# Second mixer of a two-layer transformer block: latent normalisation in two parts, modulation pieces spread over the projections, scan parts ahead of the score maxima

## The reference, cut to what matters

```
def odd_mixer(t, w_in, ...):                       # t: 256 x 1024
    proj = t @ w_in                                # 256 x 704: u 256, c_q 256, c_kv 128, k_r 64
    y_c = s5_ssm(u, ...)                           # scan over 256 tokens, 1024 complex states
    y_d = mla_attention(c_q, c_kv, k_r, ...)
    return concatenate([y_c, y_d], -1) @ w_out

mla_attention:
    q  = rmsnorm(c_q, q_norm) @ w_uq               # 256 x (6 heads x 192)
    kv = rmsnorm(c_kv, kv_norm) @ w_ukv            # 256 x (6 heads x 256)
    ... rope on 64 of the query's columns and on k_r; softmax attention, 6 heads, 2 blocks of 128 queries
s5_ssm:
    bu = u @ bbar; x_t = a * x_(t-1) + bu_t; y = Re(c x) + d u; z = gelu(y); z * sigmoid(z @ w_glu + b)
```

## Time and profile before

| what | before |
|---|---|
| median of 3 runs | 2066.13 us |
| the profiled execution's own time | 2075.66 us |
| its span | 2073.9 us |
| TensorE matmul busy | 1913.7 us (92%) |
| GpSimd / ScalarE / VectorE busy | 1347.5 / 930.1 / 722.7 us |
| memory read | 342.03 MB, 165 GB/s over the span |
| mean granted TensorE clock | 0.968 |

### The profile page before, as it was taken

How to read it: one execution, slowest core, us unless ns; L and a number is a source line. 1 busy time by engine, 2 the same in 40 slices (tenths; PEclk the granted TensorE clock), 3 DMA queues, 4 the chain that set the end, 5 groups by cost and what they waited for, 6 DMA issues and landing times.

```text
span 2073.9 us, 28300 instructions
## 1 busy us (share of the span) xinstructions
PE 1913.7 (92%) x9582; PEld 1518.0 (73%) x9582; DVE 722.7 (35%) x1296; ACT 930.1 (45%) x1458; POOL 1347.5 (65%) x780
## 2 busy tenths in 40 slices
PE   7987999889899999888999999899999999899997
PEld 5666788765678878666888776678887776678886
DVE  1375443265421134344111545342113544342112
ACT  5535344443544353544444444544444444544442
POOL 5405899440488869545988783367885883367884
PEclk9999999999999999999999999999999999999999
DMA  7666555547765546323775452245754452245552
GB/s 260 226 215 229 183 184 188 166 152 250 241 216 183 187 137 189 106 94 120 203 212 183 141 169 86 72 142 167 209 189 134 153 162 82 72 138 157 185 189 72
DMA packets 257208, 344.32 MB, mean 166 GB/s; under 512 B 33376, under 2 KB 153056, under 8 KB 257120
## 3 DMA queue, kind: packets, MB, share of 16 engines
q1 hardware_dynamic: 243328, 337.13, 50.8%
q10 hardware_dynamic: 13792, 6.03, 1.7%
HBM read 342.03 MB, written 1.05 MB: 165 GB/s over the span
## 4 chain that ended last, share of the span: by engine, by line
PE 86%; DVE 7%; ACT 2%; DMA 2%; issue 2%; SPq 0%; POOL 0%; ACTq 0%; DVEq 0%
PE bank L1930 24%; PE bank L1932 23%; PE bank L1931 23%; PE bank L2001 3%; PE bank L2450 2%; PE bank L2477 2%; PE bank L2460 2%; PE bank L2012 1%; PE bank L1980 1%; DMA raw<-in_w_mod 1%; PE bank L2167 1%; PE bank L2442 1%; DVE arena L1872 1%; PE bank L2247 1%; DVE small L1838 1%
## 5 line engine op out<-in xcount | busy, mean ns | idle before, releaser
L641 POOL TENSOR_TENSOR wl<-raw,wh 128x1024 fp32r<-128x1024 f32 x300 | 726.1, 2431 | 104.1 <-ACT wh L800 97.9
L1930 PE MATMUL bank<-wh,xh 128*128 128x512 f32 (+2 forms) x1746 | 698.8, 400 | 65.8 <-issue 30.1
L626 POOL TENSOR_TENSOR wl<-raw,wh 128x512 fp32r<-128x512 f32 (+2 forms) x238 | 319.4, 1342 | 595.6 <-ACT wh L662 558.4
L1932 PE MATMUL bank<-wl,xh 128*128 128x512 f32 (+2 forms) x1746 | 682.9, 391 | 0.0
L1931 PE MATMUL bank<-wh,xl 128*128 128x512 f32 (+2 forms) x1746 | 682.0, 391 | 0.0
L800 ACT ACTIVATE wh<-raw 128x1024 fp32r<-128x1024 f32 x270 | 286.5, 1062 | 454.9 <-PE bank L1932 433.5
L1930 PEld LDWEIGHTS bank<-wh,xh 128*128 128x128 f32 x1746 | 335.3, 192 | 145.3 <-issue 56.9
L1932 PEld LDWEIGHTS bank<-wl,xh 128*128 128x128 f32 x1746 | 335.0, 192 | 69.2
L1931 PEld LDWEIGHTS bank<-wh,xl 128*128 128x128 f32 x1746 | 335.7, 192 | 63.3 <-issue 0.7
L662 ACT ACTIVATE wh<-raw 128x1024 fp32r<-128x1024 f32 (+2 forms) x268 | 275.1, 1048 | 217.2 <-PE bank L1932 163.8
L627 POOL TENSOR_TENSOR wl<-raw,wh 128x512 fp32r<-128x512 f32 (+2 forms) x238 | 318.8, 1339 | 0.0
(11 more groups left out here) (316 smaller groups left out, 1669.5 us busy)
## 6 DMA issues: line engine op xcount, KB each, us to landing
raw<-in_w_ffn_in SPq DMA_DIRECT2D x264, 256.0 KB, 3.0
raw<-in_w_in SPq DMA_DIRECT2D x224, 256.0 KB, 2.9
raw<-in_w_mod SPq DMA_DIRECT2D x192, 256.0 KB, 3.9
raw<-in_w_ffn_out SPq DMA_DIRECT2D x132, 256.0 KB, 2.9
raw<-in_l_w_gate SPq DMA_DIRECT2D x88, 256.0 KB, 3.7
raw<-in_l_w_up SPq DMA_DIRECT2D x88, 256.0 KB, 4.4
raw<-in_l_w_down SPq DMA_DIRECT2D x88, 256.0 KB, 2.9
raw<-in_l_w_in SPq DMA_DIRECT2D x48, 256.0 KB, 4.2
```

Source lines behind the costliest of these rows:

```text
L626: nc.gpsimd.tensor_tensor(wl[:, s, 0:h], raw[:, s, 0:h], words(wh)[:, s, 0:h], ALU.subtract)
L641: nc.gpsimd.tensor_tensor(wl[:, s, :], raw[:, s, :], words(wh)[:, s, :], ALU.subtract)\
L1930: mm(dst, x_hi, w_hi, start=first, stop=False, skip_group_check=True)
L1932: return mm(dst, x_hi, w_lo, start=False, stop=last, skip_group_check=True)
```

## The change

Four things change in the second mixer; the rest of the program is as it was.

1. The latents are normed in two parts. The queries' latent (256 columns, all within the first column tile of `in1`) gets its squares, root, scaling, transposes and split before the second column tile of `in1` is taken; the keys' latent (128 columns) follows behind `uq`'s second tile. Its PSUM bank is now bank 5 (before bank 3).
2. Of the nine pieces of `mod1_rope`, six now stand one behind each chunk of `uq` and `ukv`; three are left, and they stand between the sixth and the seventh turn.
3. ScalarE converts the weights of `uq` and `ukv` in between the copies out of PSUM, no longer all ahead of them, and `c_neg` comes behind the keys' latent.
4. VectorE's loop takes its scan part ahead of `mla_top(u + 2)`; the first scan part comes before the split of the keys' latent. On TensorE `drive(2)` stands before the keys' latent is waited for, and `state(0)` behind the first chunk of `ukv`.

```diff
--- before.py
+++ after.py
@@ -230,9 +230,10 @@
     plan.modulation("mod1_in", 1, w_mod[1], 4)
     plan.gemm("in1", a["l1_w_in"], [512, 192])
     plan.modulation("mod1_lat", 1, w_mod[1], 3)
-    plan.gemm("uq", a["l1_w_uq"], [384] * 3)
-    plan.gemm("ukv", a["l1_w_ukv"], [512] * 3)
-    plan.modulation("mod1_rope", 1, w_mod[1], 9)
+    each = {n: (1, w_mod[1]) for n in range(3)}
+    plan.gemm("uq", a["l1_w_uq"], [384] * 3, modulated=each)
+    plan.gemm("ukv", a["l1_w_ukv"], [512] * 3, modulated=each)
+    plan.modulation("mod1_rope", 1, w_mod[1], 3)
...
@@ -410,7 +411,7 @@
         scratch, modbank = bank[6], bank[7]
...
-        lat_bank, ut_bank, drive_bank, state_bank, mla_out = bank[2:4], bank[0], [bank[6], bank[4]], bank[5], bank[3]
+        lat_bank, ut_bank, drive_bank, state_bank, mla_out = (bank[2], bank[5]), bank[0], [bank[6], bank[4]], bank[5], bank[3]
         accb = [[bank[0], bank[1]], [bank[2], bank[3]]]
         gub, gub0 = bank[4:6], bank[0:2]
 
@@ -926,28 +927,41 @@
...
             hi_until(plan.tiles["in1"][1][2][0][0] + RING)
-            for b in range(4):
+
+            def evac_b(b):
                 act.wait_ge(b_tr, b + 1)
                 for i in range(2):
                     nc.scalar.activation(bt[i][:, 2 * b:2 * b + 2, :],
                                          b_bank[b][:, 256 * i:256 * i + 256].rearrange("p (a b) -> p a b", a=2),
                                          ACT.Copy).then_inc(b_ev, 1)
+
+            def latent_root(i):
+                act.wait_ge(lat_ss, i + 1)
+                nc.scalar.activation(lsd[:, 2 * i:2 * i + 2], lsq[:, 2 * i:2 * i + 2], ACT.Sqrt, scale=1.0 / (256, 128)[i],
+                                     bias=eps6).then_inc(lat_std, 1)
+
+            def evac_latent(i):
+                act.wait_ge(lat_tr, i + 1)
+                for k in ((0, 1), (2,))[i]:
+                    nc.scalar.activation(xf[:, k // 2, 256 * (k % 2):256 * (k % 2) + 256],
+                                         lat_bank[i][:, 256 * (k % 2):256 * (k % 2) + 256], ACT.Identity,
+                                         scale=V_("q_norm", k) if k < 2 else V_("kv_norm", 0), bias=zero).then_inc(lat_ev, 1)
+
+            for b in range(3):
+                evac_b(b)
+            latent_root(0)
+            evac_b(3)
+            evac_latent(0)
+            act.wait_ge(ssm_ut, 1)
+            nc.scalar.activation(uT1, ut_bank[:, :].rearrange("p (a b) -> p a b", a=2), ACT.Copy).then_inc(ssm_uev, 1)
+            latent_root(1)
+            tail("in1")
+            hi_until(plan.tiles["uq"][1][2][0][0] + 1)
+            evac_latent(1)
             act.wait_ge(c_in, 32)
             nc.scalar.activation(cz[1], cz[1], ACT.Copy, scale=-1.0).then_inc(c_neg, 1)
-            act.wait_ge(ssm_ut, 1)
-            nc.scalar.activation(uT1, ut_bank[:, :].rearrange("p (a b) -> p a b", a=2), ACT.Copy).then_inc(ssm_uev, 1)
-            tail("in1")
-            act.wait_ge(lat_ss, 1)
-            nc.scalar.activation(lsd[:, 0:2], lsq[:, 0:2], ACT.Sqrt, scale=1.0 / 256, bias=eps6).then_inc(lat_std, 1)
-            nc.scalar.activation(lsd[:, 2:4], lsq[:, 2:4], ACT.Sqrt, scale=1.0 / 128, bias=eps6).then_inc(lat_std, 1)
-            hi_until(plan.tiles["uq"][1][2][0][0] + 1)
-            act.wait_ge(lat_tr, 1)
-            for k in range(3):
-                nc.scalar.activation(xf[:, k // 2, 256 * (k % 2):256 * (k % 2) + 256],
-                                     lat_bank[k // 2][:, 256 * (k % 2):256 * (k % 2) + 256], ACT.Identity,
-                                     scale=V_("q_norm", k) if k < 2 else V_("kv_norm", 0), bias=zero).then_inc(lat_ev, 1)
-            tail("ukv")
             for i in range(3):
+                hi_until(plan.tiles["uq"][i][2][0][0] + RING)
                 act.wait_ge(chunk_used, plan.tiles["uq"][i][2][-1][0] + 1)
...
@@ -970,6 +984,7 @@
                 ins.then_inc(mla_ev, 1)
 
             for i in range(3):
+                hi_until(plan.tiles["ukv"][i][2][0][0] + RING)
                 act.wait_ge(chunk_used, plan.tiles["ukv"][i][2][-1][0] + 1)
...
@@ -1556,26 +1571,34 @@
 
             row_norm("mix1", X)
             take("in1", 0, lambda t, p: v.tensor_copy(proj[:, t, 0:512], p))
-            take("in1", 1, lambda t, p: v.tensor_copy(proj[:, t, 512:704], p))
-            dve.wait_ge(evac, plan.tile_no["in1"] + 2)
-            parts = [(256, 512), (512, 640)]
-            for i, (s, e) in enumerate(parts):
+
+            def latent_squares(i):
+                s, e = ((256, 512), (512, 640))[i]
+                dve.wait_ge(evac, plan.tile_no["in1"] + i + 1)
                 for t in range(TT):
                     x = proj[:, t, s:e]
                     ins = v.tensor_tensor_reduce(q1[:, t, 256 * i:256 * i + e - s], x, x, 1.0, 0.0, ALU.mult, ALU.add,
                                                  lsq[:, 2 * i + t:2 * i + t + 1])
-                    ins.then_inc(lat_ss, 1) if (i, t) == (1, TT - 1) else step(ins)
-            dve.wait_ge(lat_std, 2)
-            step(v.reciprocal(lrs, lsd))
-            settle()
-            for i, (s, e) in enumerate(parts):
+                    ins.then_inc(lat_ss, 1) if t == TT - 1 else step(ins)
+
+            def latent_rows(i):
+                s, e = ((256, 512), (512, 640))[i]
+                dve.wait_ge(lat_std, i + 1)
+                step(v.reciprocal(lrs[:, 2 * i:2 * i + 2], lsd[:, 2 * i:2 * i + 2]))
+                settle()
                 for t in range(TT):
                     x = proj[:, t, s:e]
                     v.tensor_scalar(x, x, lrs[:, 2 * i + t:2 * i + t + 1], None, ALU.mult).then_inc(lat_xn, 1)
+
+            settle()
+            latent_squares(0)
+            latent_rows(0)
             dve.wait_ge(lat_ev, 2)
             split(0, 2, xf[:, 0, :], xt_split)
-            dve.wait_ge(lat_ev, 3)
-            split(2, 1, xf[:, 1, 0:256], xt_split)
+            take("in1", 1, lambda t, p: v.tensor_copy(proj[:, t, 512:704], p))
+            settle()
+            latent_squares(1)
+            latent_rows(1)
 
             def state_space():
 
@@ -1613,7 +1636,10 @@
                     yield
 
             ssm = state_space()
-            for _ in range(6):
+            next(ssm)
+            dve.wait_ge(lat_ev, 3)
+            split(2, 1, xf[:, 1, 0:256], xt_split)
+            for _ in range(5):
                 next(ssm)
             dve.wait_ge(xt_split, split_at["lat1"] + 2)
             dve.wait_ge(evac, plan.tile_no["uq"] + 3)
@@ -1645,11 +1671,11 @@
             for u in range(2 * MH):
                 dve.wait_ge(at_exp, u + 1)
                 v.reciprocal(rinv[:, u % 4:u % 4 + 1], rsum[:, u % 4:u % 4 + 1]).then_inc(at_rinv, 1)
-                if u + 2 < 2 * MH:
-                    mla_top(u + 2)
                 next(ssm)
                 if u % 4 == 3:
                     next(ssm)
+                if u + 2 < 2 * MH:
+                    mla_top(u + 2)
                 if u >= 3 and u % 2:
                     h = u // 2 - 1
                     dve.wait_ge(at_pv, h + 1)
@@ -2255,35 +2281,45 @@
             tile_chunk("in1", 1, 0)
             pe.wait_ge(b_ev, 2)
             b_turn(3)
-            tile_chunk("in1", 1, 1)
-            pe.wait_ge(evac, plan.tile_no["in1"] + 1)
+
+            def latent_turn(i):
+                pe.wait_ge(lat_xn, TT * (i + 1))
+                for k in ((0, 1), (2,))[i]:
+                    for t in range(TT):
+                        ins = tr(lat_bank[i][:, 256 * (k % 2) + P * t:256 * (k % 2) + P * t + P],
+                                 proj[:, t, 256 + k * P:256 + k * P + P], ident)
+                ins.then_inc(lat_tr, 1)
+
+            latent_turn(0)
             pe.wait_ge(b_ev, 4)
             turn(ut_bank, lambda i, t: proj[:, t, i * P:i * P + P], ssm_ut)
+            tile_chunk("in1", 1, 1)
             modulate("mod1_lat")
             pe.wait_ge(ssm_uev, 1)
             pe.wait_ge(b_ev, 8)
             drive(0)
-            pe.wait_ge(lat_xn, 2 * TT)
-            for k in range(3):
-                for t in range(TT):
-                    ins = tr(lat_bank[k // 2][:, 256 * (k % 2) + P * t:256 * (k % 2) + P * t + P],
-                             proj[:, t, 256 + k * P:256 + k * P + P], ident)
-            ins.then_inc(lat_tr, 1)
+
+            def latent_chunk(name, i, shift=0):
+                tile_chunk(name, i, 0, shift)
+                mod_chunk(plan.tiles[name][i][2][0][0] + 1)
+
+            x_ready("lat1", 1)
+            latent_chunk("uq", 0)
+            latent_chunk("uq", 1)
+            latent_turn(1)
             drive(1)
+            pe.wait_ge(evac, plan.tile_no["uq"] + 1)
+            latent_chunk("uq", 2)
+            drive(2)
             x_ready("lat1", 2)
             for i in range(3):
-                if i == 2:
-                    pe.wait_ge(evac, plan.tile_no["uq"] + 1)
-                tile_chunk("uq", i, 0)
-            drive(2)
-            pe.wait_ge(c_neg, 1)
-            pe.wait_ge(c_in, 32)
```

(10 more changed lines are left out.)

## The result

| | before | changed |
|---|---|---|
| median | 2070.07 us (20 runs, 2064.29 to 2081.81) | 2062.51 us (20 runs, 2052.64 to 2075.14) |
| ratio | | 0.9961, 95% interval 0.9943 to 0.9979 |
| the profiled execution's own time, span | 2075.66, 2073.9 us | 2064.33, 2062.5 us |

The changed kernel is faster by 0.39%, 8.1 us on 2070.07, and the interval is 4.3 to 11.8 us. By the two medians the gain is 7.6 us. The three runs of before that were known had a median of 2066.13; with seventeen more it is 2070.07.

A forecast was written before the change was run, and what follows sets the result against it. It took TensorE as the bound, with time won only from its waits and half clock. Before the loop 12.9 us less 3.7 + 1.7 + 0.1 gave 7.4, the loop 2.4: 9.8 us, median 2056.3, range 2051 to 2061.5.

The forecast's parts named there:

- Pieces spread: `mod1_rope`: slots freed early remove TensorE's three waits for pieces, 4.7 us, and the lower clock with them, 2.2 us.
- The new wait: TensorE waits at `uq`'s third chunk, converted only behind keys' latent and `c_neg`: plus 3.7 us, bounds 2.1 to 4.6.
- The clock behind it: Lower clock after the wait at `uq`'s third chunk: plus 1.7 us, bounds 0 to 3.3; sign, 2 to 4 us half clock.
- Rival A: At `uq`'s third chunk the clock holds or the chain is shorter: 1.7 to 4 us more gain, 2052 to 2055; 15%.
- Latents in two parts: Before `uq`: TensorE's waits for scaled latents and split go, minus 4.3 us, and the lower clock behind them, minus 1.7.
- The cover of the rotary part: Turns 6 and 7, reached about 466, find VectorE through the rotary part at about 460; no wait.
- The loop: VectorE's scan ahead of the maxima, minus 2.4 us: 0.85 off pass 8's wait, 1.6 from `state(5)` at full clock.
- B: Order moves the loss to waits at the second chunk, `ukv` or loop maxima: 3 to 6 us less gain, 2059 to 2062; 14%.
- C: Most of the gain from spreading pieces is none in undisturbed runs: no change that can be told, 2062 to 2068; 5%.
- D: Loads of `uq` and `ukv` queue on SyncE behind pieces awaiting slots: slower, four chunks cost 13.6 us, 2070; 4%.
- F: Loads of pieces aren't issued earlier, so the 4.7 us wait only stands elsewhere: 2061, chance counted in B.
- E: Transposes and short pieces before the first scores bring the lower clock: 3.2 us, 2059.5; 5%.

The follow-up runs named there:

- e1_ahead: Changed kernel with `c_neg`, the copy of `uq`'s first tile and the third chunk's conversion moved ahead of the keys' latent: 2057.28 us, ratio 0.9945 to before.
- e2_cneg: Changed kernel with `c_neg` alone moved ahead of the second root: 44.57 us from the `b_turn` transposes to the first scores, against 44.97 with the change.
- e3_conv: Changed kernel with the conversion of `uq`'s third chunk alone moved ahead of the keys' latent: 41.90 us up to the first scores, against 44.97.
- e7_nine_together: Changed kernel with the nine pieces of `mod1_rope` in one row again: 48.86 us up to the first scores, against 44.97 with the change.
- e9b_no_latents: Kernel before with pieces spread, conversions between copies and the new loop order, so the change without its latents part: 2061.11 us, ratio 0.9957.
- e6_spread_only: Kernel before with only the pieces spread and ScalarE's conversions between the copies: 42.63 us up to the first scores (before 49.90), loop 49.80.
- e8_rows: Kernel changed as in e1_ahead, with the six spread pieces in two rows of three: 2053.07 us, ratio 0.9927 to before.
- e4_loop_old: Changed kernel with VectorE's old loop order, maxima of u + 2 ahead of the scan part: loop 49.80 us, against 48.28 with the change.
- e5_loop_only: Kernel before with VectorE's new loop order alone: loop 48.29 us (before 51.49), 49.65 us up to the first scores.

## Why the prediction was right or wrong

**The level was wrong.** I said 2056.3, range 2051 to 2061.5; 2062.51 lies 1.0 us above it. The step that failed is "2056.3 for the median": I took 9.8 us from 2066.13, the median of three runs, as if it were known to a microsecond, and put nothing for it into the range. Twenty runs of the same kernel reach from 2064 to 2082 and have their median at 2070.07; the kernel before measured beside the experiments had medians of 2068.82, 2070.36 and 2068.85 (17, 15 and 23 runs). From 2070.07 the same gain would have given 2060.3, with a range that takes in 2062.51. Of the 6.2 us between forecast and result 3.9 are that level, 2.2 the size of the gain by the two medians (7.6 against 9.8). The profiled execution, at 2075.66, lay within the spread of before; I noted the 9.5 us and did not draw the conclusion that three runs close together tell little.

**The gain was right in sign and nearly in size**: 9.8 us forecast, 8.1 in the ratio, interval 4.3 to 11.8, and 8.1 in the traces. In its sum the term that was mis-sized most is "Pieces spread, minus 4.7 and 2.2 us": 6.9 forecast, 3.9 measured. The loop gave 0.8 more than forecast, which hid a part of that. The parts:

*The new wait.* Forecast 3.7 us at `uq`'s third chunk behind the keys' latent, `c_neg`, conversion and remainder; it is 4.12, in two traces. e1_ahead, e2_cneg and e3_conv show each link. 0.3 of the missing 0.4 is GpSimd: 2.5 us for its pair where I took 2.2. `c_neg` cost 0.1 less than I took (0.95 to the next row's start), and some 0.2 are the handovers between the engines, for which the sum had nothing: GpSimd's second half ends at 448.23, TensorE starts at 448.37.

*The clock behind it.* Forecast 1.7 us, measured 2.6. I took what a stretch of four microseconds had cost before; here it was six, more than the 2 to 4 us that I gave as a sign. Rival A, that the clock holds, is out: it fell behind the long wait in all five traces that have one of 3.4 us or more.

*Latents in two parts.* The terms were 6.0 away and 5.4 to come, so 0.6 gained; e7_nine_together gives 1.0 and e9b_no_latents 0.9, in single traces; against e6_spread_only, where the clock held, the part loses 2.3. Of the 1.0 in e7_nine_together 0.8 is only the lower clock at the pieces, which cost 2.2 us in the trace of before and 1.4 there. A part that removes 4.3 us of waits is worth little, since it makes a new one of the same size with the lower clock behind it.

*Pieces spread.* Forecast 6.9 us, measured 3.9 (e7_nine_together against the change; e9b_no_latents against before gives 4.0). The waits for pieces went, all of them, as said. The term that I left out is the alternation: I cost six pieces at 0.47 us each, and standing alone each costs 0.24 more, 1.4 in all (e8_rows). 0.9 us more is the clock: without the pieces the lower level behind the third chunk is shorter (0.68 over 5.34 us in e7_nine_together, 1.7 us, against 2.6). The last 0.7 is what there was to win: with the nine pieces together the lower clock cost 2.2 us in the trace of before, but in e7_nine_together only 1.4, 0.5 at the last piece (476.05 to 477.06, 1.01 us in place of 0.47) and 0.9 at the last eight transposes (1.97 us in place of 1.09).

*The cover of the rotary part.* Held, but by less than I said: `state(0)` now comes behind the first chunk of `ukv`, VectorE waited 5.36 us for it at its second spin-out and was through the rotary part near 467, not 460. TensorE reached the seventh turn at 469.44.

*The loop.* Forecast 2.4, measured 3.2: pass 8's wait went from 1.91 to 0.69 us (about 1.1 forecast), and the clock holds. Of this only 1.5 us belong to the order (e4_loop_old), where I had 0.85 for it and 1.6 for the clock; the clock behind pass 8's wait fell in the trace before and not in two others with the same wait.

*The other rivals.* B (the order moves the loss): part of the gain did go, but to alternation and clock, not to waits at the second chunk or at `ukv`, of which there are none. C and D: the interval of the gain, 4.3 to 11.8 us, leaves both out; 2062.51 lies among C's times only by the level. Once ScalarE was no longer in its way, it waited 0.76 us for a chunk's load (e1_ahead), and TensorE still didn't. F: the loads of the pieces are asked for earlier, and the 4.7 us are gone from S1 and the loop. E (the turns cost the clock): 454.40 to 471.30 with all 32 transposes is at 1.00. The Trainium skill (TensorE: Matmul & The Clock Gate, Part 4) says that transposes don't engage the full clock; here a clock that was already full wasn't lost by 24 of them in a row (2.7 us) and eight more, and whether a longer row keeps it, or brings it, no run here shows.

## What to carry to other kernels

When a wait on an in-order engine is removed, look at what is queued on the helper engines behind the step that now comes last, and move ahead what needs nothing from it: here three moved steps gave another 6.4 us of S1, where the change itself had given 4.9. Prefetch in a ring needs slots freed early, not an alternation with every product; here one row of three between the two projections was enough, and it saved 1.4 us of switching. And before a median of three runs is used as a level, ask how wide single executions spread.

## What the runs showed of the hardware

- **The clock falls behind some waits and not behind others of the same size.** Behind 3.47 to 4.12 us with full work ahead it fell each time (five traces), and so it did behind 2.78 and 2.79 us (before, e5_loop_only with 0.70 over 5.71 us, e9b_no_latents). Behind 1.83 us (e3_conv) it fell, behind 2.10 (e6_spread_only) not. In pass 8 it fell behind 1.91 us before and held behind 1.90 and 1.91 in e4_loop_old and e6_spread_only. Two traces of one stretch, with waits of 2.10 and 2.78 us, differ by 2.7 us for the clock.
- **VectorE and GpSimd slow each other.** The split's subtraction of 128 x 256 numbers takes 1.11 us beside GpSimd in e9b_no_latents and 0.42 alone in e6_spread_only, where GpSimd began later (at 447.14) because a load came late; that is the 0.7 us between the waits of 2.78 and 2.10. Before and e5_loop_only, where GpSimd also works beside it, have 1.12 us. The other way round, a half of 128 x 384 takes GpSimd 0.99 us with VectorE idle (e1_ahead, 447.50) and 1.45 beside VectorE's spin-out (the changed kernel, 446.78). GpSimd's and VectorE's rows of e9b_no_latents, then VectorE's of e6_spread_only:

```profile
436.31 0.99 POOL L627 TENSOR_TENSOR wl<-raw,wh 128x384 fp32r<-128x384 f32 x1 [2.37 <-ACT wh L663]
436.47 1.11 DVE L1168 TENSOR_TENSOR xl<-xf,xh 128x256 fp32r<-128x256 f32 x1
```

```profile
446.21 0.42 DVE L1168 TENSOR_TENSOR xl<-xf,xh 128x256 fp32r<-128x256 f32 x1
```

- **A short group of matmuls between two products costs about a quarter of a microsecond** beyond its own time in a row (0.24 on average over six in e8_rows; in the changed kernel 0.57 instead of 0.47 for the piece and 0.28 instead of 0.17 for the product behind it).
